# One wide product on constants in each step of a blocked triangular inversion

## What is computed

```python
a_low = jnp.where(strict, jnp.einsum('bhnid,bhnjd->bhnij', kb, k) * decay_mat, 0.0)
eye = jnp.eye(c, dtype=jnp.float32)                      # c = 64
t_mat = lax.linalg.triangular_solve(eye + a_low, jnp.broadcast_to(eye, a_low.shape),
                                    left_side=True, lower=True, unit_diagonal=True)
w_c = jnp.matmul(t_mat, kb * jnp.exp(gc)[..., None])
u_c = jnp.matmul(t_mat, v * beta[..., None])
```

## Time and profile before

| | |
|---|---|
| plain launches, median of 3 | 3624.16 us (3623.42 to 3625.64) |
| the profiled execution, its own time | 3652.24 us |
| its span, first to last instruction | 3650.2 us |
| mean granted PE clock over the span | 0.968 of full |
| PE busy | 3454.2 us, 95% of the span |
| first solve of the delta mixer's inversion | at 2030.38 us |
| first product of the next stage | at 2083.69 us |

### The profile page before, as it was taken

How to read it: one execution, slowest core, us unless ns; L and a number is a source line. 1 busy time by engine, 2 the same in 40 slices (tenths; PEclk the granted TensorE clock), 3 DMA queues, 4 the chain that set the end, 5 groups by cost and what they waited for, 6 DMA issues and landing times. The chain is left out here.

```text
span 3650.2 us, 52599 instructions
## 1 busy us (share of the span) xinstructions
PE 3454.2 (95%) x21636; PEld 2817.0 (77%) x21636; DVE 1768.0 (48%) x2628; ACT 1295.5 (35%) x2096; POOL 159.2 (4%) x214
## 2 busy tenths in 40 slices
PE   7789899999999899999999989999999999999997
PEld 5687787788877587788877868788878767878886
DVE  5635653444444753444466354444452555444444
ACT  5223243322233743322234134432232574433221
POOL 0110000000000000000000200000000251000000
PEclk9899899999999999999999699999999999999998
DMA  3003131222231131222221023222232002222220
GB/s 145 23 4 108 59 137 51 89 96 99 93 107 58 40 134 56 91 96 92 92 83 54 2 81 116 70 85 100 92 119 75 36 2 94 104 78 96 92 92 35
DMA packets 42724, 289.78 MB, mean 79 GB/s; under 512 B 5475, under 2 KB 6243, under 8 KB 8860
## 3 DMA queue, kind: packets, MB, share of 16 engines
q1 hardware_dynamic: 42524, 286.92, 22.0%
HBM read 284.79 MB, written 2.12 MB: 79 GB/s over the span
## 5 line engine op out<-in xcount | busy, mean ns | idle before, releaser
L924 ACT ACTIVATE w_hi<-w_raw 128x2048 fp32r<-128x2048 f32 x112 | 214.8, 1918 | 861.6 <-PE ps L1044 445.7
L308 DVE TENSOR_TENSOR w_lo<-w_raw,w_hi 128x2048 fp32r<-128x2048 f32 x145 | 330.2, 2277 | 324.5 <-ACT w_hi L300 324.2
L1040 PE MATMUL ps<-a_x_hi,w_hi 128*128 128x512 f32 x1024 | 408.0, 398 | 7.5 <-PEq L270 7.5
L1041 PE MATMUL ps<-a_x_hi,w_lo 128*128 128x512 f32 x1024 | 405.7, 396 | 0.0
L1064 PE MATMUL ps<-mlp_u_lo,w_hi 128*128 128x512 f32 x1024 | 404.5, 395 | 0.0
L1065 PE MATMUL ps<-mlp_u_hi,w_lo 128*128 128x512 f32 x1024 | 404.5, 395 | 0.0
L1044 PE MATMUL ps<-a_x_lo,w_hi 128*128 128x512 f32 x1024 | 404.4, 395 | 0.0
L1063 PE MATMUL ps<-mlp_u_hi,w_hi 128*128 128x512 f32 x1024 | 404.4, 395 | 0.0
L414 PE MATMUL ps<-x_hi,w_hi 128*128 128x512 f32 x768 | 310.6, 404 | 24.4 <-PEq L270 17.0
L300 ACT ACTIVATE w_hi<-w_raw 128x2048 fp32r<-128x2048 f32 x145 | 274.9, 1896 | 96.5 <-PE ps L1065 41.0
L414 PE MATMUL ps<-x_hi,w_lo 128*128 128x512 f32 x768 | 308.3, 401 | 0.0
(11 more groups left out here) (568 smaller groups left out, 6121.6 us busy)
## 6 DMA issues: line engine op xcount, KB each, us to landing
w_raw<-in_weights SPq DMA_DIRECT2D x255, 1024.0 KB, 4.8
x_mem<-in_mem SPq DMA_DIRECT2D x4, 1024.0 KB, 4.9
hT<-in_x SPq DMA_DIRECT2D x1, 2048.0 KB
d_bias<-bias_rows SPq DMA_DIRECT2D x1, 2048.0 KB, 9.6
n_w<-in_cmp_w SPq DMA_DIRECT2D x1, 2048.0 KB, 7.5
out_h<-hT SPq DMA_DIRECT2D x1, 2048.0 KB, 6.3
t_xi<-in_ret_xi SPq DMA_DIRECT2D x1, 1024.0 KB, 7.2
w_raw<-in_weights SPq DMA_DIRECT2D x2, 512.0 KB, 3.3
```

Of the source, the lines that this page charges most:

```text
L308: dve.tensor_tensor(self.wlo[b % SPLIT][:, 0:width], self.raw[b % RAW][:, 0:width], self.whi[b % SPLIT][:, 0:width].bitcast(F32), ALU.subt ...
L924: act.activation(c.whi[b % SPLIT][:, :], c.raw[b % RAW][:, :], ACT.Copy).then_inc(c.hi_made.sem, 1)
L1040: pe.matmul(c.ps[:, t, :], whi[:, k, cols], x_hi[:, k, :], start=k == 0, stop=False)
L1041: pe.matmul(c.ps[:, t, :], wlo[:, k, cols], x_hi[:, k, :], start=False, stop=False)
```

## The change

`invert` gets a flag, set only for the delta mixer. With it, every `solve_x`, behind its three waits and ahead of its own products, issues one product more: the 128x128 ones as weights, the 128x128 constants as moving operand, 128 columns of output, into columns 256 to 383 of the bank that solve_x is about to write. With W = 4 the solve's own results fill columns 0 to 255 of that bank; nobody reads the new columns. The new product signals nothing and waits for nothing of its own. The first layer's inversion is not changed.

```diff
@@ -1645,7 +1645,7 @@
-def invert(c, W, aT, t, tT, am, x, multiply, mask, units):
+def invert(c, W, aT, t, tT, am, x, multiply, mask, units, keep_warm=False):
@@ -1688,6 +1688,8 @@
                 if s >= 2:
                     pe.wait_ge(x_taken.sem, x_taken.at(s - 1))
+                if keep_warm:
+                    pe.matmul(c.ps[:, s % 2, 256:256 + P], c.ones, c.masks[:, 2, :], start=True, stop=True)
                 for i in range(W):
                     for h in halves:
@@ -2544,7 +2546,7 @@
-        invert(c, H, aT, t, tT, am, x, multiply, mask, 2 * NT)
+        invert(c, H, aT, t, tT, am, x, multiply, mask, 2 * NT, keep_warm=True)
```

## The result

| | before | after |
|---|---|---|
| plain launches, median | 3624.16 us (7, 3619.43 to 3630.62) | 3636.91 us (7, 3633.25 to 3641.10) |
| ratio | | 1.0033 (95%: 1.0021 to 1.0044), 8 to 16 us slower |
| the profiled execution, its own time | 3652.24 us | 3636.91 us |
| its span, its mean granted clock | 3650.2 us, 0.968 | 3634.8 us, 0.975 |

The account below looks back on a forecast made before the run. Bound: PE at half clock in the delta inversion's steps. Full clock wins 22.6 us, less 4.4 for products and 1.2 for a low entry stretch: 17 us won, plain median 3624.2 - 17 = 3607 us, range 3602 to 3630.

Parts of the forecast that it names:

- the subtraction of 28.1 us: Whole kernel: plain median taken as 28.1 us below the profiled execution, giving 3607 us beside a profiled 3635 us.
- the 22.6 us that the change was to win: Delta inversion, first to last copy: 50.7 us before against 28.1 us all at full clock, before paying for products.
- The first rival: Delta inversion: plain launches never had the clock's fall, so the change only adds 4.4 us, 3628.5 us; chance 0.18.
- The kernel is bound by PE at half clock in the steps: Delta inversion, 2046 to 2078 us: PE busy 32.00 of 32.00 us at clock 0.50, other engines waiting for it.
- The plain mix holds the high level but does not win it back: Inversion steps: solves and updates can keep clock 1.00, but did not regain it after falling to 0.50.
- Full level gives 0.55 of the time, 1.40, 2.10 and 0.94 us a step: Delta steps at full clock: plain 1.40 from 2.56 us, with multiply 2.10 from 3.82, last level 0.94 from 1.70.
- The added product costs 0.218 us at the full and 0.425 at the low level: Each delta solve's added product, two instructions, cannot hide; 20 cost 4.4 us at full clock, 8.5 us at half.
- The 0.41 us: Product price read at the low clock: 32 instructions take 6.55 us, 0.205 each, so 0.41 us per product.
- A low stretch of 3.3 us is left at the entry: Delta inversion's entry: a half-clock stretch like the first layer's would cost 1.5 us; 1.2 us was deducted.
- Nothing else waits on them: Added products in delta solves: they signal nothing, read constants, write unread columns; ACT's copy and POOL's mask have slack.
- The third rival: Delta inversion: clock never rises before the end, all 20 products cost 8.5 us, 3632.7 us, 0.23% slower; chance 0.11.
- The profiled execution at 3635 us: Whole profiled launch: 3652.2 us less 17 us won in the delta inversion, 3635 us.

Follow-up runs that it names:

- same_kernel: The kernel before the change, unedited, launched and profiled again; median 3623.68 us, ratio 1.0001.
- late_start: Kernel before, with four delta multiplies issued ahead of all steps and seven extra POOL operations delaying step 0, no added product; 3651.79 us, ratio 1.0077 to before.
- multiply_ahead: Kernel before, with the multiplies of the delta inversion's first four steps issued ahead of all steps, no added product; 3624.20 us, ratio 0.9991 to before.
- late_start_wide: As late_start, plus the change's wide 128x128 product in each of the 20 steps; 3658.11 us, ratio 1.0074 to before.
- two_narrow: Changed kernel with the added product replaced by two 64x64 products on 128 columns, one per half; 3628.66 us, ratio 1.0010 to before.
- two_wide: Changed kernel with two wide 128x128 products instead of one ahead of each delta solve; 3642.37 us, ratio 1.0047 to before.
- one_column: Changed kernel with the added product's moving operand cut from 128 columns to one; 3665.58 us, ratio 1.0106 to before.
- filled_entry: Kernel before, plus five pairs of 64x64 products ahead of PE's waits for POOL's masks at the delta inversion's entry; 3623.78 us, ratio 0.9996 to before.
- first_layer_only: Changed kernel with the added product moved from the delta mixer's inversion to the first layer's 20 steps; 3623.76 us, ratio 1.0003 to before.

## Why the prediction was wrong

The step that failed is the subtraction of 28.1 us, by which the median of the plain launches lies below the profiled execution, from both kernels alike. Those 28.1 us were for the most part the low level itself: the profiled launch of before was one of the few, about 4 in 91, that stay low. The profile of same_kernel has no such low stretch: 29.2 us between the first and the last copy, not 50.8. So in nearly every plain launch the 22.6 us that the change was to win were not there, and only the products' price was left. The first rival is what held. The second error is the price of the product.

- *The kernel is bound by PE at half clock in the steps*: right for the profiled launch, wrong for the usual one (full level from 3.4 us after the fall on).
- *The plain mix holds the high level but does not win it back*: right, as late_start shows. In same_kernel the level came back in the first steps, which hold a multiply; that the multiplies bring it back is not shown, as multiply_ahead had no fall to recover from, and in the profile of before it stayed low through all four of them.
- *Full level gives 0.55 of the time, 1.40, 2.10 and 0.94 us a step*: measured 1.40, 2.18 and 0.93 us.
- *The added product costs 0.218 us at the full and 0.425 at the low level*: wrong, 0.58 and 0.92 us. The earlier trace rows show such a product in a row of its own kind, which is not the place that it got. Twenty cost 11 us instead of 4.4 (10.6 between the copies). The 0.41 us were not wholly of the low level either: the stretch from 2008 to 2014.6 has a granted clock of 0.56.
- *A low stretch of 3.3 us is left at the entry*: right, 3.2 us in the profile after.
- *Nothing else waits on them*: right; in the plain steps after, ACT, DVE and POOL wait for PE alone and PE for none of them.
- *The first rival, 3628.5 us*: the mechanism was right and its price was mis-sized by the same term; with 0.58 us it gives 3624.2 + 11.6 = 3636 us, and 3636.9 was measured. I gave it 0.18 and spoke against it that three launches lie within 2.2 us. That was an argument for it: three launches agree with each other and lie 28 us from the profile, nearly the 22.6 us of the low level, so the profile is the odd one. I also put it to a cost that a profile has of its own. In the eleven experiments with one group of launches the profiled execution lies 3.5 us under to 5.1 us over the median, so such a cost can't be 28 us.
- *The third rival, that the product is too thin to raise the level*: it exists too, in half of the launches of late_start_wide. Its price there is twice what I gave. The changed kernel's own seven launches, at mean clocks of 0.974 to 0.976, show nothing of it. By the prediction's own figures it would have decided for slower from 19 low steps on, and not from about 17.
- *The profiled execution at 3635 us*: 3636.9. That it is so close is luck. Between first and last copy the inversion took 50.8 us in the profile of before and 39.8 in that of after, so it gives 11.0 of the 15.3 us between the two and not 17, because the product is dearer. The other 4.3 us lie ahead of the inversion, where the two kernels are the same: its first copy is at 2031.15 us in one and at 2026.82 in the other, and already in the first layer's inversion the first copies are at 158.59 and 153.72. Two profiles of kernels that are alike up to there differ as much (158.57 in same_kernel, 153.59 in two_narrow), so this is a difference between launches.

What the Trainium skill says of weight loads (TensorE: Matmul & The Clock Gate, Part 3, what overlaps and what doesn't), that they run beside products under way only where those are in other row groups, would make the wide load wait for the narrow products, and theirs for it. The same rule would hold for the second wide product of two_wide, whose load goes to the rows of the first, and that one costs 0.22 us. So the rule by itself doesn't give the 0.36 us, and no run here parts the waiting for the load from the rest. The Trainium skill (TensorE: Matmul & The Clock Gate, Why this matters for your kernels) advises to keep TensorE busy without a break to get the full clock. The traces don't agree that this is enough: PE was busy 39.00 of 39.00 us (late_start) and 85.50 of 88.30 us (one_column) at the low level. The Trainium skill (TensorE: Matmul & The Clock Gate, Part 1, the clock gate) has the monitor run freely beside the program; launches that differ at equal code fit that.

What stays open: what makes one launch in some 20 miss the recovery. In the profile of before the fall lies 0.5 us behind the start of the first solve (2030.9 against 2030.38), in same_kernel it lies at the start of the steps (2030.5), but two profiles are no proof. Open too is why some profiles have no fall at the entry at all (two_narrow, two_wide).

## What to carry to other kernels

Set the profiled execution's time and mean clock beside the plain launches before arguing from it: where they differ by as much as the effect in question, the profile may show the rare case. A filler product (one that is issued only to keep the engine's clock up) should have the tile form of its neighbours: 0.22 us against 0.58. It belongs into time in which the engine waits anyway, ahead of the wait and not behind it; in filled_entry it cost nothing that way, though nothing measurable was won either. A busy PE is not yet a PE at full clock, and a filler can lose the clock as well as hold it: with the pair all ten late-started launches got it back, with the wide product five of ten, and with a product of one column it stayed away in all four (one_column, without the late start).

## What the runs showed of the hardware

- A float32 product 128x128 on 128 columns costs 0.22 us next to its like and 0.58 us between 64x64 ones at the full level, 0.92 us at the low level, and 0.71 us with a single column there.
- Of the 0.58 us 0.36 are paid once for a group of wide products between 64x64 ones; two 64x64 products on the same 128 columns cost 0.22 us there (two_wide, two_narrow).
- With PE hardly ever idle the granted clock stayed at 0.50 for 88 us (one_column: busy 85.50 of 88.30 us), and for 46.00 us of 46.00 busy from 2034 to 2080 (late_start_wide).
- The same stream of 64x64 products holds 1.00 once it is there (same_kernel, 2034 to 2056) and stays at 0.50 when it begins there (late_start).
- In the later steps with a multiply of the first layer's inversion PE loses up to 0.8 us (3.7 to 4.2 us a step against 3.27), and the trace names only its own issue. The queue that carries instructions moves one packet of 16 KB in about each such step (same_kernel, 186 to 196 us):

```profile
DMA packets 2, 0.03 MB, mean 3 GB/s; under 512 B 0, under 2 KB 0, under 8 KB 0
q8 instruction: 2, 0.03, 1.5%
```

That PE there waits for its instructions to be fetched is a guess from this, and it was not tested. Against a plain limit on how fast they come speaks first_layer_only: its steps hold four instructions more, and they are shorter than those of 3.94 us, without such a wait.
